# The key stage of a decoder step: pages ahead of the next unit's weights in SyncE's queue

## What is computed

```python
proj = x @ w_in_l                       # 2048 -> 7184 columns
q, k, v, beta, g = dn_prep(short_conv(x_pad, conv_w), ...)
oa, S = gated_delta_chunked(q, k, v, beta, g)          # prompt
past_k = k_pool[page_table].reshape(B, -1, H_MOBA, HEAD_DIM)
kbl, vbl, kmean = moba_blocks(k_full, v_full)
gate = jnp.einsum('bqhd,bhnd->bhqn', qf, kmean)        # picks blocks
```

## Time and profile before

| what | value |
|---|---|
| median of three runs | 1550.68 us |
| the profiled execution | 1550.67 us |
| its span in the profile | 1548.9 us |
| mean granted TensorE clock | 0.993 of 2.4 GHz |
| PE busy | 1504.1 us, 97% |
| DVE busy, ACT busy | 913.6 us, 647.6 us |
| the key stage in the span | about 62 to 368 us |

### The profile page before, as it was taken

One profiled execution on the slowest core, in us unless ns is written; L12 is line 12 of the kernel. 1 busy time (PEld: TensorE's weight loads), 2 busy tenths in 40 slices (PEclk: granted clock), 3 DMA queues, 4 the chain that ended last, 5 costly groups with the idle time before them and its releaser, 6 DMA issues.

```text
span 1548.9 us, 36648 instructions
## 1 busy us (share of the span) xinstructions
PE 1504.1 (97%) x15464; PEld 1456.2 (94%) x15464; DVE 913.6 (59%) x1217; ACT 647.6 (42%) x769; POOL 90.7 (6%) x126
## 2 busy tenths in 40 slices
PE   7999999999999999999999999999999999999996
PEld 7999898989889999987999999999999999999995
DVE  4444646468743467763886666666666544445566
ACT  5444343434425444554544344543333332333434
POOL 0000000002244001001000000000000000000000
PEclk9999999999999999999999999999999999999998
DMA  8799779795678967547545454556766655555453
GB/s 305 275 370 346 291 296 362 281 390 207 253 280 322 348 243 260 201 166 264 196 164 181 172 187 166 190 177 216 270 230 245 217 181 174 188 178 176 163 181 117
DMA packets 72528, 365.11 MB, mean 236 GB/s; under 512 B 9073, under 2 KB 10426, under 8 KB 45658
## 3 DMA queue, kind: packets, MB, share of 16 engines
q1 hardware_dynamic: 56962, 310.00, 55.9%
q0 software_dynamic: 13664, 52.31, 9.1%
q10 hardware_dynamic: 1792, 1.20, 0.3%
HBM read 353.20 MB, written 10.47 MB: 235 GB/s over the span
## 4 chain that ended last, share of the span: by engine, by line
PE 87%; DVE 5%; ACT 3%; issue 2%; DMA 2%; SPq 1%; ACTq 0%; DVEq 0%
PE psum_g L556 24%; PE psum_g L557 24%; PE psum_g L558 24%; PE M L2252 4%; DVE wl L540 2%; PE M L2408 1%; PE M L556 1%; PE M L557 1%; PE M L558 1%; ACT wh L535 1%; PE psum_g L2614 1%; PE M L2267 1%; PE M L2277 1%; DMA pj<-x_t 1%; DMA raw<-w_out_t 0%
## 5 line engine op out<-in xcount | busy, mean ns | idle before, releaser
L556 PE MATMUL psum_g<-xh,wh 128*128 128x264 f32 (+1 forms) x2382 | 694.1, 291 | 5.5 <-issue 2.2
L558 PE MATMUL psum_g<-xh,wl 128*128 128x264 f32 (+1 forms) x2382 | 676.8, 284 | 1.7 <-issue 1.7
L557 PE MATMUL psum_g<-xl,wh 128*128 128x264 f32 (+1 forms) x2382 | 677.4, 284 | 0.0
L540 DVE TENSOR_TENSOR wl<-raw,wh 128x2048 fp32r<-128x2048 f32 (+1 forms) x205 | 461.6, 2252 | 287.1 <-ACT wh L535 286.5
L535 ACT CAST wh<-raw 128x2048 fp32r<-128x2048 f32 (+1 forms) x221 | 414.6, 1876 | 240.5 <-PE psum_g L558 201.7
L556 PEld LDWEIGHTS psum_g<-xh,wh 128*128 128x128 f32 x2382 | 450.2, 189 | 16.9 <-issue 12.3
L557 PEld LDWEIGHTS psum_g<-xl,wh 128*128 128x128 f32 x2382 | 450.6, 189 | 5.4 <-issue 5.2
L558 PEld LDWEIGHTS psum_g<-xh,wl 128*128 128x128 f32 x2382 | 448.8, 188 | 0.0
L556 PE MATMUL psum_g<-gh,wh 128*128 128x264 f32 x704 | 200.4, 285 | 0.2 <-DVE wl L540 0.2
L558 PE MATMUL psum_g<-gh,wl 128*128 128x264 f32 x704 | 199.4, 283 | 0.0
L557 PE MATMUL psum_g<-gl,wh 128*128 128x264 f32 x704 | 199.4, 283 | 0.0
(11 more groups left out here) (474 smaller groups left out, 1694.9 us busy)
## 6 DMA issues: line engine op xcount, KB each, us to landing
raw<-w_t SPq DMA_DIRECT2D x88, 1024.0 KB
raw<-w_in_t SPq DMA_DIRECT2D x53, 1024.0 KB
kring<-cache_k_t SPq DMA_DIRECT2D x96, 512.0 KB, 6.2
sraw<-cache_k_t SPq DMA_DIRECT2D x32, 512.0 KB, 7.0
raw<-w_out_t SPq DMA_DIRECT2D x16, 1024.0 KB
raw<-w2a_t SPq DMA_DIRECT2D x16, 1024.0 KB
raw<-w2b_t SPq DMA_DIRECT2D x16, 1024.0 KB
raw<-w2c_t SPq DMA_DIRECT2D x16, 768.0 KB
```

The costliest lines, as they stand in the source:

```text
L540: eng.tensor_tensor(wl[:, u % 2, 0:nk], raw[:, u % 2, 0:nk], wh[:, u % 2, 0:nk].bitcast(F32), ALU.subtract).then_inc(raw_used, 1)
L556: nc.tensor.matmul(out, hi_w, x_hi(k), start=(k == order[0]), stop=False)
L557: nc.tensor.matmul(out, hi_w, x_lo(k), start=False, stop=False)
L558: last = nc.tensor.matmul(out, lo_w, x_hi(k), start=False, stop=(k == order[-1]))
```

## The change

In a turn of SP's loop the request for the weights of unit u+1 now stands behind the pages of the bursts that are scored behind unit u, and behind the reading of the next page numbers. Nothing else is changed; the same transfers go to the same places with the same waits.

```diff
             load_unit(sp, turn, 0, mixer_tile(0))
             for u in range(KEY_UNITS):
-                load_unit(sp, turn, u + 1, mixer_tile(u + 1))
                 for j in bursts_at(u):
                     if j >= 2:
                         load_pages(j, pages)
                         pages = numbers(j + 1)
+                load_unit(sp, turn, u + 1, mixer_tile(u + 1))
             turn_out, n_out = STAGES["out"]
```

## The result

| | before | after |
|---|---|---|
| median, us | 1551.28 (1548.36 to 1551.98, 4 runs) | 1568.53 (1567.39 to 1572.39, 4 runs) |
| ratio, 95% interval | | 1.0126 [1.0112, 1.0140] |
| profiled execution, us | 1550.67 | 1567.39 |
| its span, us | 1548.9 | 1565.6 |

The change costs 17.3 us by the medians of the runs made side by side and 16.7 us by the two profiled executions. The ratio in the table is estimated from all runs and is not the quotient of the two medians (1.0111); by it the cost is 19.5 us, between 17.4 and 21.7. The forecast was 1567.4, a cost of 16.7.

The account below looks back on a forecast made before the run. The prediction took PE's own work as the bound (busy 1504.1 of 1548.9 us). Double bursts 14.1, first units 1.6 and to and fro 1 sum to 16.7 us, giving 1567.4 us, range 1559 to 1579.

Parts of the forecast that it names:

- The main term: Double bursts, units 18 and 26: late weights stall PE ahead of units 19 and 27, 14.1 us with what follows.
- POOL's part: Unit 19: POOL's `decays`, behind ACT's late rounding, come after PE wants them, 0.2 us more.
- the slow stretch at unit 19: Behind the stall PE's clock runs at 0.50; 1.7 us lost, up to 3.4 if it lasts twice as long.
- The first units: Units 3 to 5: transfers don't keep up with PE, so weights come late; 1.6 us, between 0.8 and 3.
- The to and fro: Units 12 to 15, 20 to 23, 28 to 31: late lowering, 0.08 us on each of 12 units, 1 us.
- "Issue" waits: Key-stage PE waits put down to no late tile, with slow stretches 8.1 us; change taken as 0, with 4 either way.
- behind the key stage: After the key stage PE is just as full, so nothing gives the loss back; 0 us.
- the weights of unit 20: Also late for ACT, about 241, but ACT is done by 243, 3 us sooner than PE needs it; no loss.
- A: Rival: small delays cascade through nearly every unit with a burst, 27 to 30 us, about 1579 us; 17%.
- B: Rival: weights overtake or share with the pages, so double bursts lose less; 5 to 9 us, about 1558; 12%.
- C: Rival: faster than before, the "issue" waits go and the double bursts stall less than 8 us; about 1546; 3%.
- D: Rival: nothing is seen, the weights' lateness is hidden everywhere by other work; 1550.7 us; 3%.

Follow-up runs that it names:

- e2: Kernel before, with weights behind the pages only in the turns of units 18 and 26; measured 1563.76 us, ratio 1.0096.
- e1: Changed kernel, but weights first again in the turns of units 18 and 26; measured 1565.05 us, ratio 1.0104.
- e3: Changed kernel, but in the turns of units 18 and 26 the weights go between the two page bursts; measured 1565.76 us, ratio 1.0111.
- e4: Kernel before, with pages first only in the turns of units 11 to 16, 19 to 24 and 27 to 31; measured 1563.01 us.
- e12: Kernel before, with weights behind pages only in turns 19 and 27, and ACT's decays there ahead of the rounding; measured 1559.07 us.
- e5: Kernel before, with pages first only in the turns of units 0 to 10; measured 1551.19 us, ratio 1.0011.
- e11: Kernel before, with weights behind pages only in turns 12 to 16, 20 to 24 and 28 to 31; measured 1554.84 us, ratio 1.0028.

## Why the prediction was right, and where it only came out so

**The main term held.** "4.7 us lost" at unit 19 measured 4.64, "5.6" at unit 27 5.65; POOL's part 0.33 (forecast 0.2); the slow stretch at unit 19 3.4 us, so 1.7 lost. From the start of unit 19 to that of unit 20 the kernel after took 1.90 us longer than before, where the sum had 1.9. Reading when a page *can* be asked for, setting the weights behind it, and adding the 11.2 us and 4.25 us of the rows gave the stall to a tenth, though PE had lost 4 us in the units ahead by then. e2 shows the mechanism alone. Only the slow stretch at unit 27 was longer than taken: 4.5 us of it lay on work, 2.3 instead of 1.7.

**The first units held:** 1.2 for 1.6, in units 3, 4 and 9 instead of 4 and 5. Which units are late changes from trace to trace (e1, whose turns 0 to 10 are those of after, has 0.40, 0.74, 0.67 and 0.26 us ahead of units 3, 4, 5 and 9), so the sum of 1.2 to 2.1 us is what held, not the units. That each small wait of PE also gives the queue time would explain why 0.8 a unit was too much; this is argued, not shown.

**The to and fro was mis-sized:** 1 us forecast, 6.5 measured (the bounds were 0 to 10). "0.08 us on each of 12 units" took an average where the loss comes as few waits, and had no clock term. In unit 15 DVE shows it (timeline of after):

```profile
194.21 2.36 DVE L578 TENSOR_TENSOR wl<-raw,wh 128x1024 fp32r<-128x1024 f32 x2 [2.13 <-ACT wh L535]
...
198.52 0.28 DVE L1560 TENSOR_SCALAR chain<-M 32x128 f32<-32x128 f32 x1
```

In the earlier trace rows the same lowering began at 192.38 and the scaling at line 1560 at 197.03: 1.8 and 1.5 us sooner. The 0.38 us of slack was right, PE's "half of a scoring, about 1 us, as cover" too thin, and 1.23 us of idle time were followed by 6.8 us at 0.50, so that one late lowering cost 1.23 + 3.4 us. This is the term of the sum that was mis-sized most, and that the total hides.

**"Issue" waits: 0 was wrong by 4.4,** just outside the ±4. Neither of the two slow places of before has a slow stretch in after: the first ran at full clock with the DMA engines still at 1.02 of their time, the second (265.2 to 268.0 us) at 0.78. So at the first the busy engines didn't by themselves make a slow stretch. Waits of this kind, 0.3 to 2.7 us long, recur near 170 and near 345 to 365 us in every trace, near 260 in most and near 280 in about half. Their sum in the key stage goes from 3.0 (e3, e4) to 7.7 us (e12) with no plain relation to the order of SP's requests.

The trace says more of them than "issue". Its DMA view has a queue q8 of the kind "instruction". Its row for 60 to 368 us of before, and the one for 166.5 to 169.1 us (packets, MB, share of the engines):

```profile
q8 instruction: 38, 0.62, 0.7%
...
q8 instruction: 1, 0.02, 2.4%
```

The one packet of the second row, 16 KB, began at 166.81, took 0.98 us, and PE's idle time ended at 169.09, 2.28 us behind its start. In the 14 traces of this document all 45 "issue" waits of 0.3 us or more in the key stage ended 2.2 to 2.6 us behind the start of such a packet; the waits for other engines and for pages ended anywhere from 0.05 to 15.8 us behind one. So what PE waits for there is, with little doubt, its next instructions, and not a tile. The packets took about 1 us there as elsewhere, and most of the 38 are followed by no wait. Why these few come late, and how much the change has to do with the fall from 5.0 to 3.6 us, is open: no run was made on it.

The error of this term and that of the to and fro (+5.5 and -4.4) nearly cancel, as does the -2.0 behind the key stage with the rest: that the total was nearer than its parts is luck.

**What the sum didn't see** is that its terms aren't independent. It did say that the weights of unit 20 come late and that ACT is "done with it by 243, 3 us sooner" than PE needs it. That is true only of a PE which the first stall has held back. Without that stall (e1) the same lateness costs 3.2 + 1.4 us at each double burst. For the change as made the sum is not touched; for every version with a part undone it is, which is why e1, e3 and e4 missed by 10 to 12 us (12 to 14 by the loss) while the forecast did not.

**The rivals.** *A* named small delays that add up to 27 us and more. The small delays exist, 6.5 us in after, but they don't run on from unit to unit: the stretches between the losses keep their length. *B*: the weights didn't overtake. At the first double burst the last page landed at 233.83 and the weights at 236.26, 2.43 us behind it (2.45 in the kernel before). The Trainium skill ("DMA: Bandwidth & Descriptors", Queues, rings and completion order) warns against counting on such an order; transfers of this size kept it in the places read here, which shows no guarantee. *C* and *D* fell with the two stalls. No order tried was faster than the kernel before; the two whose loss is smallest, e5 and e11, have 1.4 and 4.5 us of it.

## What to carry to other kernels

On a queue that issues in order, a request inherits the condition of everything ahead of it: before moving one behind another, compare *when each may be asked for*, not how long each takes. The request whose condition comes first, and whose consumer is nearest to running dry, belongs in front; here that was the weights, in all orders tried. And price a stall together with the work that stands behind it on each in-order engine, but don't add the prices of neighbouring stalls: undoing the first one can give back 2 us of 17 and undoing both 11.

## What the runs showed of the hardware

- A slow stretch of PE (granted clock 0.50) in the key stage was 3.4 or 6.8 us long, and the idle time ahead of it doesn't tell which: 6.8 us behind 1.23 us (unit 15), 3.4 us behind 4.64 us (unit 19 of after), and 6.8 us that began within the idle time at 5.65 us (unit 27) and at 4.65 and 4.26 us (e2). It can come behind a wait as short as 1.23 us, and it can stay away (behind 1.63 us, at 170.2 us of after).
- Filling PE's idle time with products that nobody reads (5.4 us of them) kept the clock at 1.00, and the time didn't fall: what PE needed next, POOL's decays, came 7.6 us behind the weights with and without them.
- All 45 waits of PE of 0.3 us or more that the profile puts down to "issue" in the key stage of the 14 traces ended 2.2 to 2.6 us behind the start of a 16 KB packet of the queue "instruction".
